# Half of a two-request encoder's probability transposes moved to the DMA crossbar

## The chip, the cores and the metric

The kernel runs on one core of a Trainium2 chip. The metric is the device time of one execution in microseconds (us). TensorE does the matrix products and, before the change, all transposes; VectorE, ScalarE and GpSimd do the elementwise work; SyncE (SP) issues the DMAs.

## The reference

Two requests, 512 and 1024 tokens of width 1024, pass through two layers with shared weights and a final RMSNorm. One layer, cut to what matters:

```python
h = rms_norm(x, g_norm) * (1 + scale) + shift
q_lat, kv_lat, k_rope, z_a, q_b, k_b, v_b, z_b = split(h @ w_in)
# group A: 8 latent heads (q, k of 96, v of 64); group B: 8 grouped-query heads of 64 on 2 key heads
def one(qblk):                                   # 128 query rows at a time
    s = einsum('bkgqd,bksd->bkgqs', qblk, k) * scale
    p = softmax(s, axis=-1)
    return einsum('bkgqs,bksd->bkgqd', p, v)
x = x + gate * (concat([oa * silu(z_a), ob * silu(z_b)]) @ w_out)
```

## The kernel before, in words

The program goes through four stages of requests: (layer 0, short), (layer 0, long), (layer 1, short), (layer 1, long). In the code `q` counts them, `r` is the request (0 short, 1 long), `S` its tokens, `NT` its tiles of 128 tokens (4 and 8), `nr` its blocks of 512 keys (1 and 2). A stage first has key steps (`key_step`), which make keys and values of all tokens, and then `NT` query tiles (`tile`), each with 16 slots, one for each head: slots 0 to 7 are the latent heads, 8 to 15 the grouped-query ones.

In slot h TensorE transposes head h's probabilities (`turn`, float32, four 128x128 blocks per 512 keys, into PSUM banks 4 and 5), multiplies the scores of head h+2 (`scores`, three products of float16 parts for a latent head, two for a grouped-query one), and multiplies the transposed probabilities of head h-1 with V (`mix`, three products of 16-bit halves per 128 keys). Between these stand pieces of "side work": the query projections of the next tile, the gates, the output projection of the previous tile, in the slots that the tables `FINISH`, `GATE_A`, `OWN`, `PREPARE` name; what stands left of the bar comes before the slot's `mix`, what stands right of it after, and "/0", "/1" are halves of one product. `slots` and `completed` put the tables together for every engine. VectorE takes each head's row maximum (`row_max`, L1321 and L1324), ScalarE the exponentials (`exponentials`, L1547). A transposed block is rounded to float16 by ScalarE (`move_pt`, L1555: the high half) and its rest is formed by VectorE (`move_pt`, L1338: PSUM minus the high half, the low half). All five queues are in order, and the order is written by hand. Waits are on semaphores that count: `exp_done`, `tr_ready`, `pt_high`, `pt_low`, `pv_done`, and `mm_ready`/`mm_free` for the rounds of side work.

The DMA queue of SyncE runs through the same slots: `load_h` (L537) loads the next tile's h, `keep_w` (L426) stores the halves of the query weights in 14 slots of the short request's tiles 2 and 3, after VectorE has made them (L1156), and `side` loads and stores the rows of x. In slot 5 of the last tile, `first_rows` (L402) loads the first rows of the next stage, and in layer 0 `key_weights` (L451, L452) loads the next stage's key weights; ahead of layer 1's short request it also loads that layer's query weights (L469, L471). After the tiles `up_weights` (L459), further rows of x (L402) and the x rows for the output of the last tile (L610) are loaded.

Shared memory that the change touches: `hT[:, 1]`, one of two 4 KB buffers of h for the key steps, unused in the tiles; `xn[0]`, the buffer of x rows; `parts`, in which weights are split; `PT` and `PT_next`, the transposed halves.

Of the kernel before, what the change touches and what calls it, by code (L numbers as in the profile page):

```python
# [82 lines left out]
def slots(first, last, ada):  # L83

    parts = ([ADA] if ada else []) + [OWN]
    if not last:
        parts.append(PREPARE)
    if not first:
        parts += [GATE_A, FINISH]
# [4 lines left out]
def completed(first, last, ada):  # L94

    return [[n.split("/")[0] for n in before + after if n[-2:] != "/0"] for before, after in slots(first, last, ada)]
# [16 lines left out]
def encoder(nc, x_prompt, x_sample, c_prompt, c_sample, w_ada, b_ada, g_norm, w_in, g_qa, w_uq,  # L113
# [18 lines left out]
    tr_before = [sum(16 * tiles[p] * trounds[p] for p in range(q)) for q in range(len(inst))]  # L132

    with ExitStack() as ctx:
# [63 lines left out]
        rows_sb = hT[0:22, 1, 0, :]  # L198
        junk = sb("junk", [P, D + MIX + 2 * KVR], BF16)
# [101 lines left out]
        def side_bank(S, n):  # L301

            return (SIDE, 3)[n % 2] if 2 * S <= SMAX else SIDE
# [9 lines left out]
            "scores_ready", "max_ready", "exp_done", "tr_ready", "pt_high", "pt_low", "pv_done",  # L313
# [12 lines left out]
        def probs_buf(h, S):  # L326

            c = h % 2 * S if 2 * S <= SMAX else 0
            return probs[:, c:c + S]

        def pt(h, S, a, c):

            if 2 * S <= SMAX:
                return PT[:, a, c + h % 2 * S // P:, :]
# [32 lines left out]
        def heads(b0, i, h):  # L367

            return 16 * (b0 + i) + h + 1

# [25 lines left out]
        def _(sp):  # L396
# [124 lines left out]
            for q, (l, r) in enumerate(inst):  # L521
# [109 lines left out]

                def tile(i, first, last):
                    for h, names in enumerate(completed(first, last, q == 0)):
# [47 lines left out]
        def _(pe):  # L681
# [59 lines left out]
            for q, (l, r) in enumerate(inst):  # L741
# [4 lines left out]
                at = {}  # L746
# [59 lines left out]
                def query_product(name, i, ps, half=""):  # L806
# [39 lines left out]
                    elif name[:3] == "ada":  # L846
                        j = int(name[-1])
                        pe.wait_ge(s["ada1_loaded"], 16 * (3 * i + j + 1))
                        last = row_product(side_bank(S, rounds.now()), ADA1_N, ada1_chunk)
# [5 lines left out]
                    else:  # L855
                        c = int(name[-1])
                        if r:
# [11 lines left out]
                def side(name, i, between=0):  # L869


                    name, _, half = name.partition("/")
                    if half != "1":
                        free = 1 if short and not between else between
                        pe.wait_ge(s["mm_free"], rounds.now() - free)
                    last = query_product(name, owner(name, i), psum[:, side_bank(S, rounds.now()), :], half)
                    if half != "0":
                        last.then_inc(s["mm_ready"], 1)
                        at[name] = rounds.step()
# [18 lines left out]
                def turn(h, i):  # L898

                    pe.wait_ge(s["exp_done"], heads(b0, i, h))  # L900
                    for c in range(nr):
                        b = c if nr == 2 else h % 2

                        wait(pe, "pt_low", tr_before[q] + nr * heads(0, i, h - 1) + c - 1)
                        for j in range(4):
                            last = transpose(psum[:, T_BANK + b, j * P:(j + 1) * P],
# [3 lines left out]
                def mix(h, i):  # L910
# [5 lines left out]
                    g = (head - HEADS) // 4  # L916
                    for c in range(NT):
                        if c % 4 == 0:
                            pe.wait_ge(s["pt_low"], tr_before[q] + nr * heads(0, i, h - 1) + c // 4 + 1)
# [938 lines left out]
```

## Time and profile before

| | us |
|---|---|
| median of 3 runs | 2260.08 (2258.73 to 2260.99) |
| the profiled execution, its own time | 2257.7 |
| its span | 2255.7 |
| TensorE matmul busy | 2075.9 (92%) |
| VectorE busy | 1579.3 (70%) |
| ScalarE busy | 1025.8 (45%) |
| GpSimd busy | 810.0 (36%) |

Busy is the union of an engine's instructions. The rows further down come from this one execution.

### The profile page before, as it was taken

How to read it: one execution, taken by the hardware profiler on the slowest of the kernel's cores; microseconds unless marked ns; L12 is line 12 of the kernel's file. 1: busy time of each engine (PE TensorE's matmuls, PEld its weight loads, DVE VectorE, ACT ScalarE, POOL GpSimd, SP SyncE). 2: the span in 40 equal slices, each digit the busy share in tenths (PEclk: the TensorE clock that was granted, in tenths of full speed). 3: DMA queues.
4: the chain of work that ended last, by engine and by line, in shares of the span. 5: the costliest groups of instructions: out<-in, count | busy, mean ns of one | idle time of the engine just before them, and what ended most of it. 6: DMA issues, size and time to landing. Idle time of an engine off the chain costs nothing.

```text
span 2255.7 us, 42409 instructions
## 1 busy us (share of the span) xinstructions
PE 2075.9 (92%) x17018; PEld 1291.2 (57%) x17018; DVE 1579.3 (70%) x2762; ACT 1025.8 (45%) x2238; POOL 810.0 (36%) x1343
## 2 busy tenths in 40 slices
PE   4889998898999999999988899889889999999997
PEld 1445554455666666666644555445566666666664
DVE  4668666587877777777746765748787777777774
ACT  1234345344655455555522434525365555555552
POOL 0563241385431233123046533228751233133220
PEclk7999999999999999999999999999999999999998
DMA  9812134550100000000522001346120100100001
GB/s 336 303 48 76 57 111 163 214 189 29 66 23 17 29 20 11 29 20 29 185 103 94 20 19 66 113 172 253 45 95 11 39 29 11 39 33 24 22 29 47
DMA packets 78519, 181.48 MB, mean 80 GB/s; under 512 B 7178, under 2 KB 32880, under 8 KB 78324
## 3 DMA queue, kind: packets, MB, share of 16 engines
q1 hardware_dynamic: 78326, 178.79, 22.1%
q8 instruction: 136, 2.23, 0.4%
q14 instruction: 57, 0.47, 0.1%
HBM read 130.50 MB, written 39.88 MB: 76 GB/s over the span
## 4 chain that ended last, share of the span: by engine, by line
PE 67%; DVE 24%; ACT 3%; DMA 2%; issue 2%; SPq 1%; POOL 0%; DVEq 0%; ACTq 0%; POOLq 0%
PE psum L702 31%; PE psum L684 11%; PE psum L693 7%; PE psum L695 7%; PE psum L694 7%; PE psum L923 5%; DVE nmax L1321 4%; DVE region L1338 3%; DVE hT L1027 2%; DVE region L1272 1%; ACT region L1531 1%; DVE PT_next L1338 1%; DVE nmax L1324 1%; ACT region L1547 1%; DVE region L1298 1%
## 5 line engine op out<-in xcount | busy, mean ns | idle before, releaser
L684 PE MATMUL psum<-ident,region 128*128 128x128 f32 (+2 forms) x3224 | 444.0, 278 | 53.2 <-DVE region L1347 13.8
L684 PEld LDWEIGHTS psum<-ident,region 128*128 128x128 f32 (+2 forms) x3224 | 359.3, 140 | 110.9 <-issue 47.9
L1321 DVE TENSOR_REDUCE nmax<-psum 128x1 f32<-128x1024 f32 (+1 forms) x384 | 397.8, 1036 | 6.7 <-PE psum L702 6.3
L1338 DVE TENSOR_TENSOR region<-psum,region 128x512 f16<-128x512 f32 x384 | 251.6, 683 | 140.4 <-ACT region L1555 140.1
L1555 ACT ACTIVATE region<-psum 128x512 f16<-128x512 f32 x384 | 214.2, 592 | 261.4 <-PE psum L684 260.8
L1610 POOL TENSOR_TENSOR region<-region,rope_sb 128x64 f32<-128x64 f32 (+3 forms) x384 | 162.2, 444 | 317.2 <-DVE region L1277 307.2
L1555 ACT ACTIVATE PT_next<-psum 128x512 f16<-128x512 f32 x256 | 139.0, 594 | 272.8 <-PE psum L684 272.8
L1547 ACT ACTIVATE region<-psum,nmax,scalars 128x1024 f32<-128x1024 f32 (+1 forms) x192 | 204.6, 1066 | 113.3 <-DVE nmax L1324 111.9
L702 PE MATMUL psum<-KTa,region 96*128 96x512 f16 x960 | 243.7, 385 | 9.6 <-DVE region L1205 9.6
L1547 ACT ACTIVATE region<-psum,nmax,unscale 128x1024 f32<-128x1024 f32 (+1 forms) x192 | 204.6, 1066 | 102.5 <-DVE nmax L1324 101.7
L702 PE MATMUL psum<-Wq,hT 128*128 128x512 f32 (+1 forms) x512 | 202.6, 542 | 0.0
L1338 DVE TENSOR_TENSOR PT_next<-psum,PT_next 128x512 f16<-128x512 f32 x256 | 165.4, 682 | 42.5 <-ACT PT_next L1555 41.9
L693 PE MATMUL psum<-Wq,hT 128*128 128x512 f16 (+1 forms) x512 | 180.9, 353 | 8.3 <-DVE region L1284 4.6
L1424 ACT ACTIVATE junk<-region 128x64 bf16<-128x64 f32 (+3 forms) x300 | 87.8, 300 | 207.5 <-DVE region L1223 136.8
L695 PE MATMUL psum<-Wq,hT 128*128 128x512 f16 (+1 forms) x512 | 180.4, 352 | 0.0
L694 PE MATMUL psum<-Wq,hT 128*128 128x512 f16 (+1 forms) x512 | 180.4, 352 | 0.0
L702 PE MATMUL psum<-region,hT 128*128 128x416 f32 x384 | 148.4, 542 | 25.4 <-DVE hT L1027 23.3
L702 PE MATMUL psum<-KTb,region 128*128 128x512 f16 x640 | 170.7, 381 | 0.0
L1610 POOL TENSOR_TENSOR scalars<-scalars 128x1 f32<-128x1 f32 x32 | 5.4, 192 | 423.4 <-ACT region L1547 423.4
L702 PEld LDWEIGHTS psum<-KTa,region 96*128 96x128 f16 x960 | 93.2, 99 | 97.5 <-issue 25.7
L702 PEld LDWEIGHTS psum<-Wq,hT 128*128 128x128 f32 x512 | 93.6, 190 | 75.3 <-issue 71.7
L1272 DVE SCALAR_TENSOR_TENSOR region<-region,psum 128x512 f32<-128x512 f32 x48 | 33.0, 687 | 140.6 <-ACT region L1531 140.6
(190 smaller groups left out, 3503.3 us busy)
## 6 DMA issues: line engine op xcount, KB each, us to landing
w_in_parts<-parts SPq DMA_DIRECT2D x28, 512.0 KB, 2.7
Wq<-w_in_parts SPq DMA_DIRECT2D x16, 896.0 KB, 7.0
Wq<-in_w_in SPq DMA_DIRECT2D x6, 2048.0 KB, 15.7
hT<-h_transposed SPq DMA_DIRECT2D x24, 512.0 KB, 3.3
Va<-in_w_ada SPq DMA_DIRECT2D x12, 1024.0 KB, 5.4
Wout<-in_w_out SPq DMA_DIRECT2D x4, 2048.0 KB, 10.8
h_transposed<-parts SPq DMA_DIRECT2D x16, 512.0 KB, 3.0
Wout<-in_w_out SPq DMA_DIRECT2D x16, 512.0 KB, 5.2
```

The costliest lines, as they stand in the source:

```text
L684: return nc.tensor.transpose(out, in_, ident[0:n, 0:n])
L693: nc.tensor.matmul(out, rows[:, 0, k, :], high(k), start=k == 0, stop=False)
L694: nc.tensor.matmul(out, rows[:, 0, k, :], low(k), start=False, stop=False)
L695: last = nc.tensor.matmul(out, rows[:, 1, k, :], high(k), start=False, stop=k == KD - 1)
L702: last = nc.tensor.matmul(out, lhsTs[k], rhss[k], start=k == 0, stop=k == n - 1)
L923: last = nc.tensor.matmul(out, pt(h, S, a, c)[:, 0, :], v, start=c == 0 and a + b == 0, stop=c == NT - 1 and a == 1)
L1321: last = nc.vector.reduce_max(nmax[:, h:h + 1], scores_buf(h, S), AX_X, negate=True)
L1338: nc.vector.tensor_tensor(pt(h, S, 1, 4 * c)[:, 0:4, :], psum[:, T_BANK + b, :].rearrange("p (c n) -> p c n", c=4), pt(h, S, 0, 4 * c)[:, ...
L1424: return nc.scalar.activation(junk[:, at:at + n], row, ACT.Square, scale=float(n) ** -0.5, accum_out=stat_col)
L1547: nc.scalar.activation(probs_buf(h, S), scores_buf(h, S), ACT.Exp, bias=nmax[:, h:h + 1], scale=scale, accum_out=sums[:, h:h + 1]).then_in ...
L1555: nc.scalar.activation(pt(h, S, 0, 4 * c)[:, 0:4, :], psum[:, T_BANK + b, :].rearrange("p (c n) -> p c n", c=4), ACT.Copy).then_inc(s["pt_ ...
L1610: mul = lambda out, a, b: nc.gpsimd.tensor_tensor(out, a, b, ALU.mult)
```

## The change

Heads are treated by their parity. Odd heads go the old way. For an even head ScalarE, right after the exponentials, writes a float16 copy of the probabilities into `p_rows` (in `hT[:, 1]`), VectorE writes what is left (`row_low`) beside it, and SyncE issues one DMA that transposes both halves (`turn_rows`; 128 rows x 2S columns of float16) into `PT`. The two products with V of an even and the following odd head are made together in the next even slot. Side work stands in other slots and uses PSUM bank 5 once (`q_b^T0`) and bank 4 for `out0` at the end of a stage. `key_weights` moves from slot 5 to slot 14 of the last tile.

```diff
-FINISH = {2: "y_b^T |", 11: "| out0/0", 12: "out0/1 |", 13: "| out1/0", 14: "out1/1 |"}
+  {2: "| y_b^T", 11: "| out0/0", 12: "out0/1 |", 13: "| out1/0", 14: "out1/1 |"}]
-OWN = {3: "q_b^T0 | z_b/0", 4: "z_b/1 |", 5: "q_b^T1 |", 15: "| y_a^T"}
+       {2: "q_b^T0 |", 3: "| z_b/0", 4: "z_b/1 |", 5: "q_b^T1 |", 15: "| y_a^T"}]
-PREPARE = {6: "q_lat |", 7: "| q_b/0", 8: "q_b/1 | q_lat^T", 9: "q_up0 |", 10: "q_up1 |", 12: "| q_a^T0", 14: "| q_a^T1"}
+           {6: "| q_lat", 7: "| q_b/0", 8: "q_b/1 | q_lat^T", 9: "q_up0 |", 10: "| q_up1", 12: "| q_a^T0", 14: "| q_a^T1"}]
...
+        p_rows = hT[:, 1, :, :].rearrange("p k n -> p (k n)").bitcast(F16)
...
-        def side_bank(S, n):
-            return (SIDE, 3)[n % 2] if 2 * S <= SMAX else SIDE
+        def side_bank(S, n, name, end=False):
+            if 2 * S <= SMAX:
+                return (SIDE, 3)[n % 2]
+            if end:
+                return T_BANK if name == "out0" else SIDE
+            return T_BANK + 1 if name in SHARED_SIDES else SIDE
+        def turn_bank(S, h, c):
+            return T_BANK + (h // 2 % 2 if 2 * S <= SMAX else c)
...
+        def probs_buf(h, S, last=False):
+            if 2 * S > SMAX and h % 2 == 0:
+                return parts[:, :, :].rearrange("p a n -> p (a n)").bitcast(F32)[:, 0:D] if last else xn[0][:, :]
...
+        def turned(q, i, h):
+            return tr_before[q] + trounds[q] * (HEADS * i + (h + 1) // 2)
+        def row_heads(q, i, h):
+            return HEADS * (before[q] + i) + h // 2 + 1
...  SyncE
+                def turn_rows(h, i):
+                    sp.wait_ge(s["p_low"], row_heads(q, i, h))
+                    wait(sp, "pv_done", heads(b0, i, h - 2))
+                    sp.dma_start_transpose(PT[:, :, :, :].rearrange("p a c n -> p (a c) n")[:, 0:2 * NT, :], p_rows[:, 0:2 * SEQS[r]]).then_inc(s["p_turned"], 16)
...
+                        if h % 2 == 0:
+                            turn_rows(h, i)
                         if last and h == 5 and q + 1 < len(inst):
                             first_rows(q + 1)
+                        if last and h == 2 * HEADS - 2 and q + 1 < len(inst):
                             if l < DEPTH - 1:
                                 key_weights(q + 1)
...  TensorE, mix
+                    by_dma = h % 2 == 0
+                    if by_dma:
+                        pe.wait_ge(s["p_turned"], 16 * row_heads(q, i, h))
...  TensorE, tile
-                        turn(h, i)
+                        if h % 2:
+                            turn(h, i)
...
-                        if h or not first:
+                        if h % 2 == 0 and (h or not first):
+                            mix(h - 2, i)
                             mix(h - 1, i)
...  VectorE
+                def row_low(h, i):
+                    dve.wait_ge(s["p_high"], row_heads(q, i, h))
+                    nc.vector.tensor_tensor(p_rows[:, S:2 * S], probs_buf(h, S, i == NT - 1), p_rows[:, 0:S], ALU.subtract).then_inc(s["p_low"], 1)
...  VectorE, tile, after the slot's side work
+                        if h % 2 and h + 1 < 2 * HEADS:
+                            row_low(h + 1, i)
+                        elif h % 2 and not last:
+                            row_low(0, i + 1)
...  ScalarE, exponentials
+                    if h % 2 == 0:
+                        act.wait_ge(s["exp_done"], heads(b0, i, h))
+                        wait(act, "p_turned", 16 * (row_heads(q, i, h) - 1))
+                        nc.scalar.activation(p_rows[:, 0:S], probs_buf(h, S, i == NT - 1), ACT.Copy).then_inc(s["p_high"], 1)
```

## Rows read from the trace of the kernel before

**Rows 1.** The page: busy time by engine.

```profile
PE 2075.9 (92%) x17018; PEld 1291.2 (57%) x17018; DVE 1579.3 (70%) x2762; ACT 1025.8 (45%) x2238; POOL 810.0 (36%) x1343
```

**Rows 2.** Busy time by stretch: the four runs of tiles; start:end, length, busy.

```profile
126.00:392.00 266.00, 240.97 (x1738) 136.07 (x1739) 190.24 (x347) 114.55 (x269) 92.42 (x102) 0.98 0.28 96
528.00:1133.00 605.00, 590.72 (x5992) 395.89 (x5991) 450.05 (x702) 326.86 (x664) 179.13 (x241) 1.00 0.12 44
1225.00:1480.00 255.00, 229.30 (x1548) 132.94 (x1549) 171.26 (x296) 117.04 (x273) 91.32 (x102) 0.98 0.15 52
1620.00:2225.00 605.00, 590.68 (x5989) 395.84 (x5988) 456.99 (x708) 331.63 (x674) 179.22 (x246) 1.00 0.09 31
```

**Rows 3.** Busy time by stretch: one steady tile, long and short.

```profile
752.50:830.70 78.20, 77.35 (x772) 51.49 (x771) 56.63 (x90) 39.90 (x86) 21.10 (x31) 1.00 0.06 21
1276.60:1349.10 72.50, 66.61 (x432) 38.19 (x431) 50.17 (x83) 25.74 (x68) 25.86 (x34) 1.00 0.02 8
```

**Rows 4.** Waits of TensorE over the span: total, times, longest.

```profile
PE psum L923 <- DVE region L1338: 31.0, 47, 1.4
```

**Rows 5.** The chain that ended last, in a steady long tile: start, length.

```profile
756.56 0.70 PE psum L923 x24
759.85 0.87 PE psum L684 x8
760.72 1.30 PE psum L702 x6
794.87 0.86 PE psum L702 x4
```

**Rows 6.** Instructions in order of time, ScalarE: exponentials of a steady tile's heads 10, 12.

```profile
801.06 1.21 ACT L1547 ACTIVATE region<-psum,nmax,unscale 128x1024 f32<-128x1024 f32 x1
...
808.58 1.21 ACT L1547 ACTIVATE region<-psum,nmax,unscale 128x1024 f32<-128x1024 f32 x1
```

**Rows 7.** In order of time, slots without side work in the last tile.

```profile
1103.84 1.21 ACT L1547 ACTIVATE region<-psum,nmax,unscale 128x1024 f32<-128x1024 f32 x1
...
1108.11 0.23 ACT L1547 ACTIVATION_READ_ACCUMULATOR region<-psum,nmax,unscale 128x1 f32 x1
1108.39 1.09 PE L684 MATMUL psum<-ident,region 128*128 128x128 f32 x8 [0.54 <-ACT region L1547]
1109.08 1.08 ACT L1555 ACTIVATE region<-psum 128x512 f16<-128x512 f32 x2 [0.74 <-PE psum L684]
...
1110.06 1.21 ACT L1547 ACTIVATE region<-psum,nmax,unscale 128x1024 f32<-128x1024 f32 x1
```

**Rows 8.** Groups of instructions: count, busy us, mean ns.

```profile
L1338 DVE TENSOR_TENSOR region<-psum,region 128x512 f16<-128x512 f32 x384 | 251.6, 683 | 140.4 <-ACT region L1555 140.1
L1198 DVE SCALAR_TENSOR_TENSOR parts<-hT,in_scale,parts 128x1024 f16<-128x1024 f32 x16 | 21.7, 1358 | 2.4 <-ACT parts L1485 2.4
L1156 DVE SCALAR_TENSOR_TENSOR parts<-Wq,in_scale,parts 128x1024 f16<-128x1024 f32 x28 | 36.9, 1318 | 0.0
L1555 ACT ACTIVATE region<-psum 128x512 f16<-128x512 f32 x384 | 214.2, 592 | 261.4 <-PE psum L684 260.8
L1485 ACT ACTIVATE parts<-hT,in_scale 128x1024 f16<-128x1024 f32 x16 | 18.4, 1148 | 28.9 <-DVE hT L1027 28.9
```

**Rows 9.** DMA issues: count, KB each, median us to landing.

```profile
w_in_parts<-parts SPq DMA_DIRECT2D x28, 512.0 KB, 2.7
...
hT<-h_transposed SPq DMA_DIRECT2D x24, 512.0 KB, 3.3
...
x_after_layer<-region SPq DMA_DIRECT2D x12, 512.0 KB, 2.6
...
h_transposed<-hT SPq DMA_DIRECT2D x8, 512.0 KB, 4.1
...
Wq<-in_w_in SPq DMA_DIRECT2D x6, 2048.0 KB, 15.7
...
parts<-in_w_in SPq DMA_DIRECT2D x1, 128.0 KB, 10.8
```

**Rows 10.** SyncE in order of time, end of layer 0's long request: start, length.

```profile
1097.95 0.38 SPq L451 DMA_DIRECT2D region<-in_w_in  x1
...
1105.01 6.70 SPq L471 DMA_DIRECT2D Wq<-in_w_in  x2
...
1135.91 0.43 SPq L402 DMA_DIRECT2D PT_next<-x_after_layer  x1
```

**Rows 11.** TensorE in order of time: the turn of slot 14 there.

```profile
1126.58 1.04 PE L684 MATMUL psum<-ident,region 128*128 128x128 f32 x8
```

**Rows 12.** The chain there: the last tile's output, added to x.

```profile
1142.92 0.76 DVE region L1298
```

More of the change, by code:

```diff
@@ L131, in encoder @@
     kept_before = [0, 0, tiles[1], tiles[1]]
-    tr_before = [sum(16 * tiles[p] * trounds[p] for p in range(q)) for q in range(len(inst))]
+    tr_before = [sum(HEADS * tiles[p] * trounds[p] for p in range(q)) for q in range(len(inst))]
     with ExitStack() as ctx:
@@ L867, in query_product, with side @@
                     return last
-                def side(name, i, between=0):
+                def side(name, i, end=False):
                     name, _, half = name.partition("/")
+                    bank = side_bank(S, rounds.now(), name, end)
                     if half != "1":
-                        free = 1 if short and not between else between
-                        pe.wait_ge(s["mm_free"], rounds.now() - free)
-                    last = query_product(name, owner(name, i), psum[:, side_bank(S, rounds.now()), :], half)
+                        pe.wait_ge(s["mm_free"], freed[bank])
+                        if bank == T_BANK + 1:
+                            wait(pe, "pt_low", bank_turned)
+                    last = query_product(name, owner(name, i), psum[:, bank, :], half)
                     if half != "0":
                         last.then_inc(s["mm_ready"], 1)
-                        at[name] = rounds.step()
+                        at[name] = freed[bank] = rounds.step()
                 def scores(h, i):
@@ L927, in tile @@
                 def tile(i, first, last):
-                    for h, (before_mix, after_mix) in enumerate(slots(first, last, q == 0)):
-                        turn(h, i)
+                    for h, (before_mix, after_mix) in enumerate(slots(first, last, q == 0, r)):
+                        if h % 2:
+                            turn(h, i)
                         if short:
@@ L950, in _ @@
                 scores(1, 0)
+                freed = {bank: rounds.now() for bank in (3, T_BANK, T_BANK + 1, SIDE)}
                 over_tiles(NT, tile)
-                side(EPILOGUE[0], NT)
-                between = 0
+                side(EPILOGUE[0], NT, True)
                 if q + 1 < len(inst):
                     head_done = head(q + 1)
-                    between = 2
-                side(EPILOGUE[1], NT, between)
-                side(EPILOGUE[2], NT)
+                side(EPILOGUE[1], NT, True)
+                side(EPILOGUE[2], NT, True)
                 if q == 0:
@@ L1567, in tile @@
                             exponentials(0, i + 1)
-                        if short:
+                        if short and h % 2:
                             move_pt(h, i)
@@ L1792, in tile @@
                 def tile(i, first, last):
-                    for h, names in enumerate(completed(first, last, q == 0)):
+                    for h, names in enumerate(completed(first, last, q == 0, r)):
                         if h == FINAL_SLOT and l == DEPTH - 1 and not first:
```

100 lines of the change are left out of this document (60 added, 40 removed).

## The prediction, made before the change was run

> **What bounds the kernel now.** I read the page's busy times first: TensorE 92%, VectorE 70%, ScalarE 45% [rows 1]. A mean over unlike stages says little, so next come the stretches. The four runs of query tiles take 1731 us of the 2255.7, and only they are changed directly. In a steady long tile TensorE is busy 77.35 of 78.2 us, VectorE 56.63 and ScalarE 39.9; in a steady short one it is 66.61 of 72.5, with VectorE at 50.17 [rows 2, 3]. So the long request is bound by TensorE in its steady tiles, and the short one by TensorE with gaps. The waits say whose gaps: products with V stand 31.0 us behind the low halves that VectorE makes, 47 times, nearly all in the short request [rows 4]. In slots without side work the bound is another: there TensorE's transposes wait for the exponentials, by 0.54 us in the row shown, and two slots take 1110.06 - 1103.84 = 6.2 us, of which TensorE's own work is 2 x (0.87 + 0.86 + 0.70) = 4.9 [rows 5, 7].
>
> **What is removed.** One turn of a long head (8 transposes) moves the chain by 0.87 us [rows 5]; the 1.09 of the time view includes the pipeline's end [rows 7]. 16 long tiles x 8 even heads = 128 turns x 0.87 = 111 us. A short head's turn is half of it: 64 x 0.44 = 28 us. All of it is 139 us, if TensorE bounds everywhere.
>
> **What takes its place on the other engines.** ScalarE: a long even head had two roundings of 592 ns and has one copy of 1024 columns out of SBUF instead; the nearest row is 1148 ns (L1485) [rows 8]: -0.04 us a head. VectorE: two subtractions of 683 ns against one of 1024 columns from SBUF; the nearest row takes 1358 ns (L1198) [rows 8]: the same. The short heads go from 592 and 683 ns to about half of these rows. So both engines keep their load. What changes is the load's place: the copy stands in front of the next exponentials, the subtraction in front of the next row maximum. ScalarE then has 1.08 + 2 x 1.42 + 1.15 = 5.1 us in two slots [rows 7, 8], less than the 6.2 there, so no new bound by itself.
>
> **The transpose itself.** No row shows a crossbar transpose. It moves 512 KB for a long head (256 KB short). Lower end: 2.6 us, a plain DMA of 512 KB [rows 9]. Upper end: 10.8 us, the landing of 128 KB in short pieces, the worst DMA of that kind [rows 9]. A transpose reads and writes SBUF in pieces shorter than a row, so I put it above the 3.3 and 4.1 us of the loads and stores of the same size, at 4.5 us for a long head and 3.5 for a short one, near to these rows.
>
> The rule that speaks against the change: the Trainium skill, "VectorE: DVE Perf Modes", section "The three transpose paths", gives 1309 ns for one 128x128 block of 16-bit data by DMA against 390 ns on TensorE. For the other side, "Advanced Engine Details and Errata", section "X-Bar Transpose (TRN2)", says that such DMAs are as fast as ordinary ones. A long head is 16 blocks: by the first figure taken as a rate 20.9 us, far beyond any row; by the second near the 2.6 us. No row of before decides.
>
> **The ring that it closes.** `p_rows` is one buffer. ScalarE may write head h+2's copy only when head h's transpose has landed; then come the subtraction and the next transpose. One turn of this ring is 1.15 (copy) + 1.3 (subtraction) + 0.3 to issue (0.38 for a plain one [rows 10]) + 0.2 for the three hand-overs + the transpose: 3.0 + 4.5 = 7.5 us for two long slots. TensorE's own loop, from `mix` of head h to the transpose into the same `PT` to `mix` of head h+2, is shorter: 0.7 + 0.5 + 4.5. Behind ScalarE's wait stand the next exponentials and the odd head's roundings, and TensorE waits for these; that is how the ring reaches the end.
>
> Long steady tiles, 12 (78.2 us, 8 pairs of slots, mean 9.8): each pair loses 0.87, 7.0 in a tile. The shortest pair now is 808.58 - 801.06 = 7.5 us [rows 6]; after it would be 6.65, and the ring holds it at 7.5. So 7.0 - 1.0 (that pair, and a little for hand-overs) = 6.0 a tile: 72 us.
>
> Long first and last tiles, 4: some three pairs in each have no side work. They take 6.2 [rows 7] and are bound by ScalarE's chain; the ring makes them 7.5, +1.3 each. The other five save 0.87 each: 4.4 - 3.9, about 0 in all.
>
> Short tiles, 8: 28 us of transposes. The products of the even heads no longer stand right behind VectorE's low halves: half of the 31.0 us [rows 4], 15. Against it: in tiles 2 and 3 `keep_w` stands in SyncE's queue ahead of the next transpose, 28 times in the two requests; it waits for VectorE's 1.32 us and moves 512 KB in 2.7 us [rows 8, 9]. The ring there is 0.6 + 0.7 + 0.5 + 3.5 + 4.0 = 9.3 against a mean pair of (266 + 255)/64 = 8.1 [rows 2], in a part of the pairs long enough already: 0.4 us each, 11. For friction between ring and side work 10. Sum 28 + 15 - 11 - 10 = 22 us. Bounds: 0 and 43.
>
> **Moved steps.** Side work in other slots: the same instructions, TensorE has work on both sides of them: nothing; if a moved piece meets an unready input it costs what the waits of its kind cost now, under 2 us a stage. The bank shared by `q_b^T0` adds a wait for low halves made a slot earlier: nothing; were it late, the products behind it would be too.
>
> `key_weights` from slot 5 to 14 counts at one place, ahead of layer 1's short request, where it also loads the query weights. Its train is issued from 1097.95 to 1111.71 [rows 10] and its last load lands 15.7 us after its issue [rows 9], so 29 us from first to last. It was over before the tiles ended. Now it starts behind slot 14's transpose, at some 1129 [rows 11], and ends at 1158; the x rows that SyncE issues at 1135.9 [rows 10], and those for the last output, which VectorE uses at 1142.9 [rows 12], queue behind it. 1158 - 1143 = 15 us late. Bounds: 0, if the queue's order hurts less, and 28, the whole shift. In layer 0's other transition only the key weights move, no cost seen.
>
> **The sum.** 72 + 0 + 22 - 15 = 79 us off the profiled execution's 2257.7: 2178.7. The median of the runs is 2.4 us above that execution, so 2181.
>
> **Rivals.**
> *The transposes are too slow and the ring sets the pace.* The mean long pair is 1210/128 = 9.45 us [rows 2]. The ring passes it when the transpose takes 6.5 us; from about there the kernel is slower than before, since the 15 us stay. At 8 us the ring is 11.0: (11.0 - 9.45) x 128 = +198, with the 15 and nothing from the short request 2473; at the upper row's 10.8 it is 13.8: +557, some 2830. For it: that row, and three engines in series on one buffer. Against: plain DMAs of the size take 2.6 to 4.1. The skill's 1309 ns a block, taken as a rate, would make a ring of 23.9 us and about 4120; the chances below count it here.
> *All of it arrives.* A transpose near the lower end, a ring of 5.6 us under every pair, and loads that land in time: 2257.7 - 139 + 2.4 = 2121. For it: TensorE at 99% in steady tiles. Against: the slots without side work, where it isn't the bound.
> *The other engines take over.* VectorE had 450 us of 605 [rows 2] and would be at 82% in the long request, in one fixed order, with a subtraction that waits for ScalarE in front of row maxima that the next scores need. If each steady pair loses 0.5 us to that, 12 x 8 x 0.5 = 48 of the 79 go: 2229.
> *The moved loads and SyncE's order cost more than the turns save.* 28 instead of 15, and each transpose held by 1 us behind other DMAs (192 us spread over pairs, half hidden): 2257.7 - 79 + 13 + 96 = 2288. For it: SyncE's queue is in order, and at slot 14 of layer 1 it waits for the final rows. Against: these waits end before the next product is due.
>
> **Chances.** Forecast (2150 to 2215) 0.43; all arrives (to 2150) 0.12; engines take over (2215 to 2255) 0.10; within 0.2%, 4.5 us either way and about what a measurement of this kernel can tell from none, 0.04; moved loads and order 0.09; slow ring 0.22. So faster 0.65, same 0.04, slower 0.31. The range 2110 to 2340 leaves out 0.02 below and most of the slow ring above; the forecast's own is 2150 to 2215.
>
> **What would show it.** TensorE's transposes fewer by 1280 and its busy time down by 139 to 170 us. A steady long tile at 71 to 73 us. The landing of the 512 KB transposes in the DMA issues: 3 to 6 us right, over 6.5 wrong. ScalarE idle before its copy until a transpose lands, in the slots without side work alone; if in all, the slow ring. TensorE's waits before products with V: on VectorE down by half, on DMAs near nothing. VectorE idle some 15 us at the start of layer 1's short request until x rows land. Wrong altogether if a long tile exceeds 78 us.

## The result, and the profile after

The changed kernel takes 2278.99 us (median of 4 runs, 2274.03 to 2284.02) against 2259.99 for the kernel before on the same chip: a ratio of 1.0087 with a 95% interval of 1.0072 to 1.0102. It is 19 us slower, not 79 us faster. The profiled execution spans 2272.0 us, 16.3 more than the span of before, 2255.7.

The first view is the page of the changed kernel: busy time by engine, the DMA packets and SyncE's queue (its last column is the share of the 16 DMA engines' time).

```profile
PE 1987.8 (87%) x15738; PEld 1168.6 (51%) x15738; DVE 1597.6 (70%) x2634; ACT 1031.8 (45%) x2110; POOL 851.7 (37%) x1343
...
DMA packets 412336, 265.25 MB, mean 117 GB/s; under 512 B 341002, under 2 KB 366704, under 8 KB 412148
...
q1 hardware_dynamic: 412150, 262.70, 43.9%
...
region<-hT SPq DMA_TRANSPOSE x192, 4.2
```

TensorE lost 88 us of work and 1280 matmuls [rows 1], and the span still grew: it idles 284 us, 180 before. The last line, from the DMA issues, is the transpose: 4.2 us in the median from issue to landing, short and long heads together.

The second view is the busy time by stretch (start:end, length, busy time and instructions by engine, granted clock, DMA share, GB/s). The four runs of tiles are now cut exactly at their exponentials; then come a steady long tile, the long request's first tile, the short request's last tile, and the way from the long tiles of layer 0 to the short ones of layer 1.

```profile
128.70:404.40 275.70, 238.78 (x1595) 130.17 (x1585) 194.56 (x344) 114.27 (x267) 91.87 (x98) 0.93 0.43 114
542.00:1127.40 585.40, 540.11 (x5384) 334.22 (x5383) 450.88 (x634) 326.59 (x596) 185.27 (x236) 0.98 0.42 84
1240.10:1504.40 264.30, 226.84 (x1404) 126.94 (x1405) 174.02 (x293) 116.37 (x270) 95.97 (x102) 0.91 0.32 79
1646.30:2239.40 593.10, 541.70 (x5385) 334.26 (x5384) 457.58 (x639) 331.30 (x606) 200.61 (x246) 0.98 0.42 87
770.70:844.70 74.00, 70.67 (x708) 43.78 (x707) 56.48 (x82) 40.22 (x78) 22.07 (x31) 1.00 0.43 81
542.00:621.50 79.50, 62.81 (x579) 38.60 (x578) 63.79 (x79) 48.06 (x83) 46.97 (x40) 0.88 0.44 108
338.10:404.40 66.30, 54.27 (x362) 27.82 (x361) 41.84 (x74) 31.73 (x59) 5.12 (x6) 0.87 0.56 155
1127.40:1240.10 112.70, 85.95 (x403) 49.15 (x401) 50.70 (x125) 20.42 (x66) 49.19 (x116) 0.86 0.54 190
```

The same cuts of the kernel before, for the last three, which [rows 2, 3] don't have:

```profile
528.20:596.00 67.80, 60.83 (x643) 42.15 (x642) 58.76 (x87) 47.73 (x92) 40.82 (x38) 1.00 0.21 79
330.90:387.70 56.80, 49.26 (x389) 27.38 (x388) 41.81 (x77) 30.84 (x58) 3.61 (x5) 0.97 0.49 169
1128.20:1225.10 96.90, 81.38 (x382) 45.95 (x379) 49.83 (x126) 20.49 (x65) 49.30 (x116) 0.96 0.32 114
```

Cut at the first and last exponentials, the tiles of before took 261.0, 600.0, 250.0 and 600.2 us. So the 16.3 us come together as follows. Twelve steady long tiles: 445.2 + 452.0 us against 2 x 469.3, -41.4. Two first long tiles: 79.5 and 77.4 against 67.8 and 68.2, +20.9. Two last long ones: -1.2. Short request: +14.7 and +14.3. The transition shown: +15.8. The rest (start, two transitions, end): -6.8. The steady long tile did get shorter, 78.20 [rows 3] to 74.00 in the view (74.2 in the mean of layer 0, 75.3 in layer 1); but TensorE, at 77.35 of 78.20 before, is at 70.67 of 74.00.

The waits of the changed kernel (engine, line, what it waited for: total us, times, longest us) name what holds it. L1617 is the copy into `p_rows`, L966 `mix`, L337 SyncE's wait for `mix` before a transpose, L660 the transpose itself.

```profile
ACT hT L1617 <- DMA region<-hT: 217.1, 149, 4.0
...
PE psum L966 <- DVE region L1382: 39.2, 35, 1.4
...
PE psum L966 <- DMA region<-hT: 34.3, 36, 2.9
```

and from SyncE's own list:

```profile
SPq L337 <- PE psum L966: 866.9, 156, 11.1
```

The waits on the DMA and SyncE's did not exist before. The second line did: it is TensorE waiting for the low halves of odd heads, 39.2 us, against 31.0 before for all heads [rows 4]; half of these 31.0 were to go. ScalarE stood 217.1 us before the copies of even heads until the last transpose had read `p_rows`, in 149 cases. SyncE, before 156 of 192 transposes, stood until TensorE had made the product of head h-2. Such a wait costs nothing by itself; the trace tells in how many cases it decided. For each even head I took the end of the subtraction (L1389, what the transpose reads) and of the product of head h-2 (what frees `PT`): the product ended later in 80 of the 184 cases inside a run of tiles, by 3.3 us in the mean, and the transpose was issued 0.08 us behind it in the median. In all 80 cases ScalarE then idled before the next copy, 100.2 us together; in the other 104 it idled 114.1 us together. So by this sorting the 217 us fall into two kinds of about one size; what each kind costs is for the experiments to show.

One case of the first kind, in order of time (start, length, engine, line; idle time before in brackets), in a steady long tile:

```profile
901.42 1.23 DVE L1389 TENSOR_TENSOR hT<-xn,hT 128x1024 f16<-128x1024 f32 x1
...
905.18 0.86 PE L966 MATMUL psum<-Vb,region 128*128 128x64 f16 x24
...
906.12 1.92 SPq L660 DMA_TRANSPOSE region<-hT  x1
...
910.91 1.06 ACT L1617 ACTIVATE hT<-xn 128x1024 f16<-128x1024 f32 x1 [0.97 <-DMA region<-hT]
```

The rows are ready at 902.65. The transpose starts at 906.12, because `mix` of head h-2 reads `PT` until 906.04, and lands at 910.9, 8.3 us behind the subtraction, though it takes only 4.8 itself.

And one turn of the second kind, in the short request's last tile:

```profile
368.49 0.52 PE L966 MATMUL psum<-Va,region 128*128 128x64 f16 x12 [1.29 <-DMA region<-hT]
368.52 0.63 ACT L1617 ACTIVATE hT<-region 128x512 f16<-128x512 f32 x1 [1.99 <-DMA region<-hT]
...
369.67 0.69 DVE L1382 TENSOR_TENSOR region<-psum,region 128x512 f16<-128x512 f32 x1 [2.60 <-ACT region L1623]
370.28 0.68 DVE L1389 TENSOR_TENSOR hT<-region,hT 128x512 f16<-128x512 f32 x1
...
370.88 1.28 DVE L1201 SCALAR_TENSOR_TENSOR parts<-Wq,in_scale,parts 128x1024 f16<-128x1024 f32 x1
...
372.18 0.38 SPq L450 DMA_DIRECT2D w_in_parts<-parts  x1
372.66 1.53 SPq L660 DMA_TRANSPOSE region<-hT  x1
...
376.51 0.63 ACT L1617 ACTIVATE hT<-region 128x512 f16<-128x512 f32 x1 [2.60 <-DMA region<-hT]
```

From 368.52 to 376.51 is 7.99 us for two short slots, 7.1 (56.8 / 8) before. It is copy 0.63; 1.13 in which VectorE, in its order, has the odd head's subtraction first, which waits for a rounding that stands behind the copy on ScalarE; subtraction 0.68; 1.70 in which SyncE's queue has `keep_w` first, whose store waits for VectorE's L1201; and 3.85 for the transpose.

The transition, on SyncE (one line was 0.38 us long at 1097.95 before [rows 10]):

```profile
1129.62 1.76 SPq L660 DMA_TRANSPOSE region<-hT  x1
1131.44 1.15 SPq L475 DMA_DIRECT2D region<-in_w_in  x1
...
1140.11 7.04 SPq L495 DMA_DIRECT2D Wq<-in_w_in  x2
1147.19 5.26 SPq L637 DMA_DIRECT2D x_after_layer<-region  x1
...
1163.01 0.43 SPq L426 DMA_DIRECT2D PT_next<-x_after_layer  x1
```

The train of weights starts at 1131.44, the x rows follow at 1163.01 instead of 1135.91, and VectorE waits 25.0 us once for the rows of L1343, ScalarE 36.3 us once for those of L1483 (8.2 us before). The train's issues end at 1147.15. Behind them stands the store of the last tile's rows (L637, at 1131.02 before), and SyncE then waits 9.5 us for that store to land before it may load the x rows, 3.3 us before.

### The profile page after: what moved, and what is told of

The parts are those of the page before. It is cut to its first block and busy times, and to the rows that moved or that the text cites. A ratio compares the mean times of both kernels' runs of the same rounds, so it can differ in the third digit from the quotient of the medians.

```text
span 2272.0 us, 40130 instructions
## 1 busy us (share of the span) xinstructions
PE 1987.8 (87%) x15738; PEld 1168.6 (51%) x15738; DVE 1597.6 (70%) x2634; ACT 1031.8 (45%) x2110; POOL 851.7 (37%) x1343
## 2 busy tenths in 40 slices
DMA packets 412336, 265.25 MB, mean 117 GB/s; under 512 B 341002, under 2 KB 366704, under 8 KB 412148
## 3 DMA queue, kind: packets, MB, share of 16 engines
q1 hardware_dynamic: 412150, 262.70, 43.9%
## 5 line engine op out<-in xcount | busy, mean ns | idle before, releaser
L717 PE MATMUL psum<-ident,region 128*128 128x128 f32 (+2 forms) x1944 | 276.5, 283 | 66.4 <-ACT region L1609 25.0
L735 PE MATMUL psum<-KTa,region 96*128 96x512 f16 x960 | 256.4, 401 | 27.0 <-DVE region L1250 18.3
L717 PEld LDWEIGHTS psum<-ident,region 128*128 128x128 f32 (+2 forms) x1944 | 222.0, 142 | 109.8 <-issue 42.6
L735 PE MATMUL psum<-Wq,hT 128*128 128x512 f32 (+1 forms) x512 | 209.8, 564 | 1.3 <-DVE region L1329 1.1
L1382 DVE TENSOR_TENSOR PT_next<-psum,PT_next 128x512 f16<-128x512 f32 x256 | 164.4, 682 | 46.0 <-ACT PT_next L1623 45.8
L726 PE MATMUL psum<-Wq,hT 128*128 128x512 f16 (+1 forms) x512 | 181.8, 355 | 16.2 <-DVE region L1335 9.8
L1483 ACT ACTIVATE junk<-region 128x64 bf16<-128x64 f32 (+3 forms) x300 | 87.0, 292 | 192.2 <-DVE region L1268 124.4
L1609 ACT ACTIVATE region<-psum,nmax,scalars 128x1024 f32<-128x1024 f32 (+1 forms) x128 | 126.1, 985 | 97.5 <-DVE nmax L1369 96.9
L1389 DVE TENSOR_TENSOR hT<-xn,hT 128x1024 f16<-128x1024 f32 x112 | 144.2, 1288 | 35.5 <-ACT hT L1617 33.3
L1609 ACT ACTIVATE region<-psum,nmax,unscale 128x1024 f32<-128x1024 f32 (+1 forms) x128 | 125.6, 982 | 94.5 <-DVE nmax L1369 94.3
L1617 ACT ACTIVATE hT<-xn 128x1024 f16<-128x1024 f32 x112 | 118.4, 1057 | 100.6 <-DMA region<-hT 99.5
L735 PEld LDWEIGHTS psum<-Wq,hT 128*128 128x128 f32 x512 | 100.9, 201 | 92.0 <-issue 81.9
L735 PEld LDWEIGHTS psum<-region,hT 128*128 128x128 f32 x384 | 75.5, 201 | 94.3 <-issue 63.0
```

What stands on the lines that cost most here:

```text
L717: return nc.tensor.transpose(out, in_, ident[0:n, 0:n])
L726: nc.tensor.matmul(out, rows[:, 0, k, :], high(k), start=k == 0, stop=False)
L735: last = nc.tensor.matmul(out, lhsTs[k], rhss[k], start=k == 0, stop=k == n - 1)
L1382: nc.vector.tensor_tensor(pt(h, S, 1, 4 * c)[:, 0:4, :], psum[:, turn_bank(S, h, c), :].rearrange("p (c n) -> p c n", c=4), pt(h, S, 0, 4 ...
L1389: nc.vector.tensor_tensor(p_rows[:, S:2 * S], probs_buf(h, S, i == NT - 1), p_rows[:, 0:S], ALU.subtract).then_inc(s["p_low"], 1)
L1609: nc.scalar.activation(probs_buf(h, S, i == NT - 1), scores_buf(h, S), ACT.Exp, bias=nmax[:, h:h + 1], scale=scale, accum_out=sums[:, h:h ...
```

## Experiments

Each ran against the kernel before on the same chip. The cuts from the code are shortened. In the variants the same lines of code have other numbers: the copy is L1669 or L1680, the subtraction L1434 or L1445, SyncE's wait for the product L357.

**The short request by TensorE.** The choice by which an even head goes through the DMA got a table of tiles.

```diff
-                    if h % 2 == 0:
+                    if h % 2 == 0 and i in DMA_TILES[r]:      # DMA_TILES = {0: (), 1: all 8}
```

> The changed kernel with the short request as before: all its heads turned by TensorE, side work in its old slots; the long request by DMA as in the change. Theory A (the short request loses because its stage never had TensorE as its only bound: the change took 14.7 and 14.3 us more in its two runs of tiles, 275.7 against 261.0 and 264.3 against 250.0): both runs of tiles go back to 261 and 250, and the kernel takes 29 us less, about 2250. Theory B (the short request is slow because of what the queues and the clock carry over from the long one): its runs of tiles stay above 270 and 260, and the kernel gains under 10 us.

Measured: 2255.76 us, ratio 0.9986 [0.9975, 0.9996]. The short request's tiles take 260.5 and 250.3 us, as before. The 23 us that return are most of what it lost (29.0); in the profile the long request of layer 1 took 600.3 us, 593.1 in the changed kernel, and no run tells why. With the long request alone changed, the kernel is level with the one before.

**Query weights late.** The loads of layer 1's query weights behind the x rows.

```diff
-                if l and r == 0:
-                    query_weights(l)
+                # at the end of the long request's tiles instead, behind load_x and the last side work
+                if q == 1:
+                    query_weights(1)
```

> The changed kernel, with layer 1's query weights (7.9 MB) issued behind the first rows of x of the short request instead of ahead of them, at the end of the stage before; the key weights stay in slot 14. Theory A (the x rows queue behind that train): the wait of ScalarE for the x rows (36.3 us in the changed kernel) falls under 10, the stretch from the last exponentials of layer 0's long request to the first of layer 1's short one goes from 112.7 back to 97, and the kernel takes 15 us less, about 2264. Theory B (the stretch is longer because TensorE runs there at the lower clock, 0.86 granted on average): the stretch stays above 108.

Measured: 2263.18 us, ratio 1.0020 [1.0010, 1.0030], 15.8 less than the changed kernel. The x rows are issued at 1141.81 (1163.01), the longest wait of ScalarE for them is 16.2 us (36.3), and the stretch takes 100.40 (112.70). That is theory A's direction and its time, but not its whole size: the wait was to fall under 10 us and the stretch to 97. SyncE still waits 7.6 us there for the store to land, 3.3 before the change. The mean granted clock in the stretch rose too (0.95, from 0.86), so a share of the clock in the gain is not excluded:

```profile
1126.00:1226.40 100.40, 82.60 (x403) 47.35 (x401) 50.45 (x125) 20.63 (x65) 49.08 (x116) 0.95 0.61 214
```

**Two buffers of rows.** `p_rows` alternates between two places; `PT` stays single.

```diff
+        p_rows_bufs = [hT[:, 1, :, :]..., parts[:, 1, :]]      # short: the two halves of hT[:, 1]
-                        wait(act, "p_turned", 16 * (row_heads(q, i, h) - 1))
+                        wait(act, "p_turned", 16 * (row_heads(q, i, h) - 2))   # long: from tile 1 on
```

> The changed kernel with two buffers for the rows that are transposed (in the long request from its tile 1 on), so that ScalarE's copy waits for the transpose before the last. Theory A (the ring of copy, subtraction and transpose sets the pace where slots are short): ScalarE's wait for the transposes, 217 us in the changed kernel, falls under 40, and the kernel takes 15 to 40 us less, about 2250. Theory B (that wait is slack, the order of the engines' queues decides): the wait goes and the time stays within 6 us of the changed kernel's 2279.

Measured: 2211.57 us (2209.84 to 2214.32), ratio 0.9795 [0.9776, 0.9813], -67 against the changed kernel, more than was expected. Its waits and two stretches (the short request's last tile, a steady long one):

```profile
ACT hT L1669 <- DMA region<-hT: 17.4, 11, 3.2
```

```profile
SPq L357 <- PE psum L1002: 909.3, 161, 12.0
```

```profile
330.50:388.10 57.60, 47.96 (x354) 24.92 (x353) 41.85 (x74) 32.02 (x58) 3.92 (x6) 0.94 0.60 172
826.60:900.10 73.50, 70.46 (x708) 43.84 (x706) 56.64 (x82) 40.54 (x78) 21.96 (x31) 1.00 0.39 80
```

ScalarE's wait is gone, SyncE's is not (909.3 us). So what costs is not that a transpose is late: it is that ScalarE stops for it, with the next exponentials behind it. The short last tile is back at 57.6. The long request's first tile, where the second buffer is not free, stays at 78.9 and 77.3 us.

**The kernel before with the loads at slot 14.**

```diff
+                        if last and h == 14 and q + 1 < len(inst):
+                            key_weights(q + 1)          # was at slot 5
```

> The kernel before with one edit: the weights of the next stage are loaded in slot 14 of the last tile instead of slot 5. Theory A (the move alone costs what the changed kernel lost between the stages): 2260 + 15 = 2275. Theory B (the loss there comes with the transposes in the DMA queue): under 2265.

Measured: 2261.08 us, ratio 1.0010 [0.9999, 1.0021]. The edit did nothing in time, so it decided nothing. The first load is issued at 1099.78, against 1097.95 [rows 10], and the tiles too end 1.8 us later. In the kernel before nothing holds SyncE between slots 5 and 14, so the place in its program is not a time. It becomes one only with `turn_rows`, whose waits hold the queue until 1129.62. The 15 us are then the price of both edits together; the changed kernel with the loads back in slot 5 was not run.

**Without the gating of Wout** (changed kernel, then kernel before). GpSimd's product of Wout with the gate is cut to 1 of 1024 columns in the long request; that part of the computation is left out.

```diff
-                    last = mul(Wout[:, k, :], Wout[:, k, :], gate)
+                    w = 1 if r else D
+                    last = mul(Wout[:, k, 0:w], Wout[:, k, 0:w], gate[:, 0:w])
```

> The changed kernel, in which GpSimd multiplies the output weights by the gate in one column of 1024 only in the long request (the rest of that product is left out), so that GpSimd hardly runs in the long request's first tile. That tile took 79.5 and 77.4 us in the changed kernel and 67.8 and 68.2 before. Theory A (VectorE's new subtraction from SBUF, 1.22 us elsewhere, runs beside GpSimd's SBUF work at up to 3.02 us, and the ring is held by it): the subtractions of that tile take 1.22 us, the tile falls under 72 us, the kernel takes over 12 us less than 2279. Theory B (the ring alone, and the tile's order of work, cost it): subtractions at 1.22 us, and the tile stays above 75.

> The same edit on the kernel before, as the measure for the run above: what GpSimd's gating costs where VectorE reads PSUM. Both theories: little, the first long tiles stay within 3 us of 67.8 and 68.2, the kernel within 6 us of 2260. If they fall by as much as in the changed kernel, neither theory on the subtraction holds.

Measured: changed 2269.65 us, ratio 1.0037 [1.0024, 1.0049], -9.3; before 2258.9, ratio 0.9995 [0.9983, 1.0007], nothing, with first long tiles of 70.3 and 68.4 us. The profile is from a second run of the changed kernel with the same edit:

> As in the run of this kernel before it, GpSimd's product of Wout with the gate is cut to 1 of 1024 columns in the long request (that part of the computation is left out); its trace is wanted. Theory A (GpSimd's work in SBUF stretches VectorE's subtraction in the long request's first tile): the subtraction there is at 1.2 to 1.3 us throughout (up to 3.02 us in the changed kernel) and the first long tiles take 72 to 75 us (79.5 and 77.4). Rival B (the subtraction is stretched by something else, such as the moved weights' DMAs or the clock): subtractions over 1.8 us remain and the tiles stay at 76 to 80 us. Time about 2270 us in both.

Measured: 2270.04 us, ratio 1.0040 [1.0027, 1.0053]. The subtractions of the first two even heads, of the changed kernel (with GpSimd's gating beside them) and then of this one, and its first long tile:

```profile
544.07 15.85 POOL L1678 TENSOR_TENSOR Wout<-Wout,region 128x1024 f32<-128x1024 f32 x6
```

```profile
544.48 3.02 DVE L1389 TENSOR_TENSOR hT<-xn,hT 128x1024 f16<-128x1024 f32 x1
...
552.97 2.44 DVE L1389 TENSOR_TENSOR hT<-xn,hT 128x1024 f16<-128x1024 f32 x1 [1.51 <-ACT hT L1617]
```

```profile
541.77 1.23 DVE L1434 TENSOR_TENSOR hT<-xn,hT 128x1024 f16<-128x1024 f32 x1 [0.44 <-ACT hT L1669]
...
548.45 1.23 DVE L1434 TENSOR_TENSOR hT<-xn,hT 128x1024 f16<-128x1024 f32 x1 [1.49 <-ACT hT L1669]
```

```profile
539.40:616.20 76.80, 58.33 (x578) 36.42 (x577) 60.46 (x78) 47.67 (x84) 28.83 (x40) 0.93 0.46 112
```

Without the gating these two subtractions are back at 1.23 us. But theory A wanted 1.2 to 1.3 us throughout the tile, and two later subtractions stay long, 2.08 and 1.80 us (1.88 and 1.81 in the changed kernel); there GpSimd has other SBUF products running. And the size is under what theory A gave: the two first tiles take 76.8 and 74.2 us, 2.7 and 3.2 less, not 72 to 75 both. The gating's part is under a third of what they lost.

**Filler matmuls.** Four needless transposes per even head on TensorE in the short request, 28 us of work in all, into a PSUM bank that nothing uses there.

> The changed kernel with the four transposes that each even head lost in the short request put back as idle work: four transposes of a constant into an unused PSUM bank, 64 x 4 in all, 28 us of TensorE at 2.4 GHz. Theory A (the short request lost time because TensorE ran at 1.2 GHz in more stretches there, granted clock 0.93 and 0.91 against 0.98): the clock goes back to 0.97 or more, and the two runs of tiles take no longer than 275.7 and 264.3, or less. Theory B (the clock is a by-product of the waits, the ring sets the pace): the fillers fit into the waits in part, the clock may rise, and the runs of tiles take 0 to 15 us more each.

Measured: 2288.71 us, ratio 1.0122 [1.0098, 1.0146], +9.7. The clock hardly rose (0.95, against 0.93, in the stretch of layer 0's tiles, which takes 279.0 us; 0.93, against 0.91, in layer 1's, 272.8 us), so the question whether a full clock would give time back is not settled by it. The time fits theory B, 0 to 15 us more in each run of tiles (3.3 and 8.5).

**Two destinations.** One buffer of rows as in the changed kernel, but `PT` and a second place in turn for the transposed halves.

```diff
-                    wait(sp, "pv_done", heads(b0, i, h - 2))
-                    sp.dma_start_transpose(PT[...], p_rows[...])
+                    wait(sp, "pv_done", heads(b0, i, h - (2 if r and (i, h) <= (1, 0) else 4)))
+                    sp.dma_start_transpose(turned_rows(q, i, h), p_rows[...])
```

> The changed kernel with one buffer of split rows, as it is, but two destinations for the transposed probabilities of even heads, used in turn (from the long request's tile 1 on the second half of the attention parts' buffer, in the short request the free half of the rows' own slot). The SyncE queue then waits for TensorE's product with V four heads back and no longer two. Theory A (the ring is held by the destination: the transpose of head h may not begin before TensorE has finished the product of head h-2): the 866.9 us of SyncE's waits for that product nearly vanish, ScalarE's copy hardly waits for the transposes (under 50 us in all, 217.1 in the changed kernel), and most of the gain of the second rows buffer comes: 2279 - 67 + up to 20 = 2212 to 2235 us. Rival B (the rows' buffer itself, read and written in turn by copy, subtraction and transpose, holds the ring): with 1.06 + 1.23 + 4.2 us of it needed for each even head and the hand-overs, ScalarE still waits for over 120 us, and the time stays at 2262 to 2279 us.

Measured: 2230.92 us (2230.05 to 2232.61), ratio 0.9872 [0.9854, 0.9891]: -49 against its control below, in the range of A.

```profile
SPq L357 <- PE psum L1013: 105.2, 56, 12.3
```

```profile
ACT hT L1680 <- DMA region<-hT: 66.5, 38, 4.1
...
ACT hT L1680 <- DMA hT<-hT: 40.5, 25, 3.1
...
ACT hT L1680 <- DMA parts<-hT: 28.5, 21, 2.4
```

```profile
758.40:830.50 72.10, 70.22 (x708) 43.86 (x707) 56.53 (x82) 40.49 (x77) 21.93 (x31) 1.00 0.40 82
```

But ScalarE still waits 135.5 us in three groups, where A said under 50 and B over 120. Sorted as above: in the cases where the product of head h-2 ends after the subtraction its idle time fell from 100.2 to 22.0 us, in the others it stayed (114.1, now 112.6). So both theories hold a part. A second place for `PT` gives 49 us back; it is no cost of `PT` by itself, for with two buffers of rows 67 us came back while SyncE still waited for that product 161 times. The rest between the two variants, some 18 us (67 - 49), lies in the short request: its tiles take 266.3 and 255.9 us here, 258.7 and 242.0 with two buffers of rows, most of it in the last tile (65.9 and 57.6). That part hangs on the rows' buffer itself.

**The first long tile by TensorE.** `DMA_TILES = {0: (0, 1, 2, 3), 1: (1, ..., 7)}` in the table above, nothing else.

> The changed kernel with the first tile of the long request (one of 8, in both layers) turned wholly by TensorE, as in the kernel before; all other tiles unchanged. If the 10 us that each of these two tiles lost come from VectorE's subtraction stretched beside GpSimd's gating and from the transposes' waits (theory A), the tile takes 68 to 71 us (79.5 and 77.4 in the changed kernel, 67.8 and 68.2 before) and the time is 2279 - 16 to 20 = 2259 to 2263 us. Rival B (the moved side work makes that tile long, whoever turns the probabilities): the tile stays at 76 to 80 us and the time at 2274 to 2280 us.

Measured: 2266.42 us, ratio 1.0025 [1.0015, 1.0035]: -14 against the control, a little under A's 16 to 20. The tile is at 70.5 (79.5), in layer 1 at 72.3 (77.4), a little above A's 68 to 71: who turns the probabilities decides most of its length, not the moved side work, which stands in its new slots here too.

```profile
544.80:615.30 70.50, 62.19 (x643) 42.47 (x641) 59.41 (x87) 47.55 (x91) 41.85 (x41) 0.98 0.18 68
```

**Control.** The changed kernel with these choices as parameters, at its own values.

> The changed kernel itself with its choices as parameters (which tiles' even heads go by DMA, how many buffers), all at the changed kernel's values: the reference for the variants. Both theories expect the changed kernel's time, 2279 us within 5, and a ratio to the kernel before of 1.0087 within 0.002. If it comes out apart from that, the variants' differences are to be counted from here.

Measured: 2280.28 us (2277.25 to 2281.68), ratio 1.0086 [1.0069, 1.0104], as expected. Its two profiled executions differ by 3 us in one stage (267.4 and 264.3 in layer 1's short tiles), so smaller differences between single stages are not read.

**The pieces together.** Two buffers of rows, late query weights, first long tile by TensorE.

> Three edits on the changed kernel: two buffers of rows, the query weights behind the x rows, and the long request's first tile wholly by TensorE. From the parts: two buffers gave 2211.6, late query weights -15.8 in the changed kernel, and the first long tile -10 each if it goes back to 68. If these are separate causes the sum is 2176 (within 8). If the first tile is slow for the order of its side work, not for the transposes, 2196. If the late weights no longer help, 2190.

Measured: 2179.12 us (2176.2 to 2179.93), ratio 0.9631 [0.9613, 0.9649]. It beats both kernels, by 81 and 100 us. Its steady long tiles take 72.4 to 73.9 us (72.2 was forecast); its short tiles of layer 0 and the first long tile:

```profile
127.50:384.40 256.90, 227.70 (x1588) 125.19 (x1577) 193.84 (x343) 115.95 (x266) 90.74 (x98) 0.96 0.45 122
523.10:592.70 69.60, 62.13 (x642) 42.91 (x641) 59.62 (x87) 47.78 (x91) 41.87 (x40) 0.98 0.18 69
```

The three pieces are nearly separate: -67, -16 and -14 in the three runs of one piece each would give 2182.

## Why the prediction was wrong

The sign is wrong: 2181 was forecast, 79 us gained, and 19 were lost (16.3 by the profiled spans). Of these 95 us between forecast and profile 51 lie in the short request, 31 in the steady long tiles, 20 in the first and last long ones and 1 in the loads; the rest of the kernel, forecast unchanged, took 7 less. By its steps:

**What is removed: right in a steady tile.** 1280 transposes fewer. But over the kernel TensorE's busy time fell by 88 us and not by 139 or more: the rows show a lower granted clock in the short request (0.93 and 0.91, 0.98 before [rows 2]) and the first long tiles, where the same matmuls take longer (a short head's product 0.52 us at full clock, 0.82 at half of it); in a steady long tile at full clock it fell by 77.35 - 70.67 = 6.7 us, against 7.0.

**The durations: right.** Copy 1.06 us (1.15 forecast), subtraction 1.23 where nothing disturbs it (1.3), transpose 4.2 to 4.3 us for a long head and 3.1 to 3.2 for a short one (4.5, 3.5). Engine loads stayed level. The slow ring as it was described (a transpose over 6.5 us) is not what happened. Of the two figures of the Trainium skill that were weighed, that of "VectorE: DVE Perf Modes", section "The three transpose paths", doesn't hold as a rate: 16 blocks take 4.2 us and not 20.9. "Advanced Engine Details and Errata", section "X-Bar Transpose (TRN2)", is near: 4.2 us against 2.6 to 4.1 of ordinary DMAs of 512 KB [rows 9].

**The ring: the step that failed.** The forecast priced a closed loop of copy, subtraction and transpose at 7.5 us, and set it aside wherever a pair of slots is longer than that. It named TensorE's loop through `PT` and dropped it because it is "shorter". Two things were missing. First, the two loops are one: a transpose starts at the later of the subtraction and the product of head h-2, and that product stands in TensorE's order in slot h, behind what TensorE has in that slot. Where TensorE is late with it, the transpose is late, then, with one buffer of rows, the copy, then the exponentials behind the copy, and time that a short pair could have made up is gone. Two destinations alone give 49 us back, and then the twelve steady long tiles gain 66 us of the 72 that were forecast (the changed kernel gained 41); two buffers of rows alone give 67 back. Second, a loop over in-order queues contains what stands in them: 1.13 us of VectorE's order and 1.70 us of SyncE's in the turn shown. Mean lengths hide it: what counts is each pair of slots and what is ahead in each queue.

**Short request: wrong in sign.** -22 forecast, +29 measured. The term of 28 us of removed transposes was credited whole, though the rows said that TensorE has gaps there. In the changed kernel nothing of it arrived, and with two buffers of rows only part: there the tiles take 258.7 and 242.0 us, 10 us less than before in all. The 15 us for products that no longer wait for low halves did not come either: the odd heads' products alone wait 39.2 us for them, 31.0 was all of it before, and 34.3 us of waits for transposes came on top, where near nothing was expected. The charge for the ring was 0.4 us a pair, 11 us in 28 pairs; the last tile alone pays (66.3 - 56.8) / 8 = 1.2 us a pair, 9.5 us, in layer 1 11.4. How much of the 29 us is the lower clock, and not the waits, is not separated: no run held the clock up.

**First long tiles: mis-sized.** About 0 was forecast, +20.9 measured. Under a third is the subtraction stretched by GpSimd's gating (below); most of the rest goes when TensorE turns the tile. How it divides between the ring and the clock was not tried: a second buffer is not free in that tile, and its clock is 0.88 where it was 1.00. With levels of 0.5 and 1.0 that is some 19 of its 79.5 us at the low one, an estimate from the row; if TensorE set the pace all that time, up to half of it, near 10 us, would be lost to the clock.

**The loads: right.** 15 forecast, 15.8 measured in the transition, and 15.8 of the whole time given back by the late query weights (12.3 of them in that stretch). The x rows queue behind the weights, as forecast, and are issued at 1163.0 where 1158 was expected; the wait for the store ahead of them to land was not in the working. The reason needed the new waits on SyncE, as the kernel before with the same edit shows.

**Rivals.** The sign that was named for the slow ring did appear: ScalarE idle before its copy in 149 of 192 cases, not in the slots without side work alone. That rival was tied to a transpose over 6.5 us, and a ring can be slow without one. "The moved loads and SyncE's order cost more" came nearest in the number: 2288 against 2279, and its 1 us for each transpose held by other DMAs was there in the turn shown (1.70), though the larger part was TensorE's product and not a DMA. "The other engines take over" was not it: VectorE is as busy as before (1597.6 us, 1579.3 [rows 1]).

## What to carry to other kernels

A handed-over stage with one buffer at its input and one at its output is one loop through all the engines' queues. Price it as the later of its two releases at every turn, with what stands ahead in each in-order queue, and not as the sum of its own instructions; and ask whether the release comes from the engine that was meant to be relieved. Before work is taken from the bounding engine, see whether a second buffer on either side can be had: here it decided between 19 us lost and 48 won. An instruction behind no wait runs early wherever it stands; a new wait ahead of it makes its place in the program a time.

## What the hardware showed that was not expected

A subtraction with both inputs in SBUF (L1389) takes 1.23 us in the steady tiles and 3.02 and 2.44 us beside GpSimd's products of Wout, also in SBUF; without these, 1.23. The subtraction of the same kind that reads PSUM and SBUF (L1382, 512 columns) takes 0.68 to 0.69 us throughout the kernel. The Trainium skill, "SBUF — State Buffer", section "SBUF: two separate sides", says that a VectorE operation with two SBUF inputs and a GpSimd operation that reads SBUF take turns on a shared pair of ports, each for its whole instruction. By that rule moving the subtraction from PSUM to SBUF exposes it; the trace agrees.

A crossbar transpose of 128 rows x 2048 columns of 16 bits lands 4.2 to 4.3 us after its issue (medians by stage), of half of that 3.1 to 3.2; the issue itself holds SyncE for 1.2 us (short) to 1.9 us (long), where a plain DMA of the kernel before takes 0.38 [rows 10]. The packets under 512 bytes go from 7178 to 341002, and the queue's share of the DMA engines from 22.1% to 43.9%.

TensorE's granted clock fell where it paused. In the short request of the changed kernel:

```profile
184.00:187.00 3.00, 0.35 (x1) 0.14 (x2) 2.90 (x6) 0.87 (x2) 2.84 (x3) 0.86 0.68 166
187.00:190.00 3.00, 2.56 (x28) 1.83 (x27) 1.90 (x5) 1.88 (x4) 2.84 (x5) 0.50 0.00 0
190.00:193.00 3.00, 3.00 (x12) 2.16 (x12) 2.19 (x4) 0.87 (x2) 2.84 (x4) 0.50 0.76 51
193.00:196.00 3.00, 2.58 (x35) 1.27 (x34) 1.37 (x3) 1.61 (x3) 2.84 (x4) 1.00 0.20 45
```

After 2.9 us without a matmul (a wait for VectorE's L1250, not for a transpose) it runs at 0.50 of full speed (1.2 GHz of 2.4) and is at 1.00 again at 193. The kernel before, busy throughout, is at 1.00 from 184 to 190. What this adds to the 29 us of the short request stays open.
